# A hybrid decoder step on one core: rows gathered in float32, the last tile's norm inside its selection, merged rows in the gates' place, buffer 5 loaded at the merge

## The chip, the cores and the metric

The kernel runs on one core of one Trainium2 chip, as one launch. The metric is the device time of one execution in microseconds. Before the change it is 1523.48 us, the median of 3 runs (1522.27 to 1524.48).

## The reference

One step of a decoder layer is computed for 256 prompt rows and 8 x 4 sample rows of width 1024, 288 rows in all, everything in float32. The two groups differ only in their states:

```
x @ w_in -> q, f, v, g, z, xBC, dt, gate_a, gate_b
out_a = (rms_norm(hgrn2 recurrence) * sigmoid(g)) @ hg_proj
out_b = rms_norm((mamba-2 recurrence + skip) * silu(z)) @ ssd_proj
merged = sigmoid(gate_a) * out_a + sigmoid(gate_b) * out_b
mix = merged @ w_out
h = layer_norm(ALPHA * x + mix, ln1_g, ln1_b)

logits = h @ router_w + router_b            # 32 experts
top 4 of them, gates = softmax of the top 4 logits
for each chosen expert: gu = h @ w_gu[e] + b_gu[e]; act = (clip(up) + 1) * min(gate, 7) * sigmoid(1.702 * gate)
                        y += gates * (act @ w_down[e] + b_down[e])
x = layer_norm(ALPHA * h + y, ln2_g, ln2_b)
```

The recurrent states and the last three rows before the convolution are outputs too. The change touches what lies between `merged` and the expert products, and the storage of the sum behind them.

## The kernel before

The program is written per engine: each engine has one list of instructions in order, and semaphores join them. An engine whose instruction waits holds up everything behind it. SyncE (SP) issues all the large transfers, on one queue, in the order in which they are written; each also waits for the semaphore that says that its place in memory is free.

Rows lie in three tiles, two of 128 prompt rows (0 and 1) and one of 32 sample rows (2). Up to about 548 us the kernel computes the projections, the two recurrences and the two branches. `gA` and `gB` hold the activated gates, transposed (features across partitions). For each of 8 feature groups the second branch's product is multiplied by `gB` (line 1612), then the first branch's by `gA`, and the sum is written over `gB`, which is called `mT` from there on (lines 1623 and 1624, semaphore `g_m`, called merged_ready).

**The mix.** TensorE multiplies the merged rows by the two halves of `w_out`, in the order of `MIX` (line 697): tile 2 first half, tile 0 first half, tile 2 second, tile 0 second, tile 1 first, tile 1 second (`mix(0)` to `mix(5)`, line 2215). VectorE's `evict(j)` (line 1639) adds ALPHA times the input row (`xres`, loaded again) and writes the sum to `xtok`; TensorE's `turn` (line 2231) transposes that sum, ACT copies it to `hTr`, and TensorE multiplies it with the router's weights (`logits`). Layer norm is folded into the router by factors, so the logits don't wait for the normed rows. The normed rows themselves come from `weigh` (subtract the mean, multiply by `lnw`) and `normal` (multiply by the inverse deviation, add `lnb`), written over `xres`. Ahead of `evict(0)` VectorE waits for the inputs (`g_xr`) and for both vectors of the norm (line 1697, `g_ln` at 32, called ln_parameters_loaded). `choose` finds the 4 experts of each row.

**The blocks.** The chosen (row, expert) pairs are sorted by expert into blocks of 64 rows, of which this input has 32. VectorE writes `psel`, a 0/1 matrix that says which row is in which place of the block; TensorE gathers a block by multiplying the rows by it. A bf16 0/1 matrix times float32 rows isn't exact in one bf16 product, so the rows are held as three bf16 parts `hp` whose sum is the row: ACT casts, GpSimd subtracts the cast from the row, ACT casts what is left, and so on. For tile 2 the three parts lie below each other in 96 partitions (`hp2`), so one product of each half is enough; tiles 0 and 1 take three. For tile 1 TensorE forms the residual itself, with a product by the identity and one by the negated identity `nidb` (lines 2285 to 2290), and VectorE forms the third part (line 1747). The two halves of the 1024 columns go to the two halves of the partitions of one PSUM bank (`gather`, line 2294).

For each block TensorE works through six pieces of 2 MB of the expert's weights: four of `w_gu` (256 rows each) and two of `w_down` (512 rows each). During piece 3 or before piece 4 it gathers the next block's rows, transposes gates, activation and rows, and in every second block, from the third on, it multiplies the pair's outputs back to their rows (`scatter`). SyncE loads the pieces into ten buffers (`buf_kb`, line 620). The first ten pieces, of experts 0 and 1, which nearly every input starts with, are loaded before the table of blocks is known: buffers 0 to 3 around the branches, 4 behind `w_out`, 6 after `mix(4)`, 5 and 7 after `mix(5)`, 8 after the logits and the normed first half of tile 1, 9 after the casts of tile 0. From the eleventh piece on, a ring of nine buffers is used, and a piece is issued when TensorE has used the one that was in its buffer (line 868, `m_f`). After the last block the sum in `yacc` is normed and stored.

The functions that the diff touches, with those that call them:

Of the kernel before, what the change touches and what calls it, by code (L numbers as in the profile page):

```python
# [14 lines left out]
BF16 = mybir.dt.bfloat16  # L15
I32 = mybir.dt.int32
U32 = mybir.dt.uint32
ALU = mybir.AluOpType
# [71 lines left out]
def build(nc, x_prompt, x_sample, state_hgrn, state_ssm, state_conv, hg_lower_bounds, w_in, hg_norm_w, hg_proj,  # L90
# [24 lines left out]
    with ctx:  # L115
# [377 lines left out]
        mT = gB  # L493
# [4 lines left out]
        lnb = at("lnb", 170, [P, D])  # L498
# [98 lines left out]
        t_c, t_r, t_q = S("h_part_cast"), S("h_residual_ready"), S("last_h_residual_ready")  # L597
        t_z = S("last_h_part_ready")
# [49 lines left out]
        hp0 = [[at(f"hp{t}{i}", kb, [P, D], BF16) for i, kb in enumerate(places)] for t, places in enumerate(((148, 150, 152), (162, 164, 114)))]  # L648
        hp2 = at("hp2", 112, [96, D], BF16)
        hres = at("hres", 183, [P, D])  # L650
        yacc = at("yacc", 154, [P, 2, D])
# [10 lines left out]
        psel = at("psel", 205.9375, [P, 3, BLK], BF16)  # L662
# [10 lines left out]
        nidb = at("nidb", 198.6875, [P, P], BF16)  # L673
# [12 lines left out]
        lnw2 = at("lnw2", 148, [P, D])  # L686
        lnb2 = at("lnb2", 162, [P, D])
        lnw4 = at("lnw4", 152, [P, 256])
        lnb4 = at("lnb4", 153, [P, 256])
# [45 lines left out]
        with nc.Block() as block:  # L735
            @block.sync
            def _(sp):
# [74 lines left out]
                sp.dma_start(lnb[:], row(ln1_b[0])).then_inc(g_ln, 16)  # L812
# [76 lines left out]
                for t in range(2):  # L889
                    for h in range(2):  # L890
                        sp.wait_ge(f_y, 2 * t + h + 2)
                        sp.dma_start(y_prompt[0, P * t:P * t + P, CW * h:CW * h + CW], yacc[:, t, CW * h:CW * h + CW]).then_inc(s_out, 16)
# [7 lines left out]
            def _(pool):  # L900
# [53 lines left out]
                pstep(g.tensor_scalar(nidb[:], ident[:], -1.0, None, ALU.mult))  # L954
# [11 lines left out]

                h2 = xres[0:96, 2, :]
                pool.wait_ge(t_c, 1)
                g.tensor_tensor(hres[0:96, :], h2, hp2[:], ALU.subtract).then_inc(t_r, 1)
                pool.wait_ge(t_c, 3)  # L970
                pool.wait_ge(t_r, 1)
                g.tensor_tensor(hres[64:96, :], hres[64:96, :], hp2[64:96, :], ALU.subtract).then_inc(t_r, 1)
                for i in range(2):
                    for n in range(2):
                        cols = slice(CW * n, CW * n + CW)
                        pool.wait_ge(t_c, 6 if i == 0 else 7 + n)
                        pool.wait_ge(t_r, 2 + 2 * i + n)
                        g.tensor_tensor(hres[:, cols], hres[:, cols] if i else xres[:, 0, cols], hp0[0][i][:, cols], ALU.subtract).then_inc(t_r, 1)
# [9 lines left out]
            def _(act):  # L988
# [213 lines left out]
                def cast(t, i, n, residual):  # L1202

                    cols = slice(CW * n, CW * n + CW)
                    act.wait_ge(t_r, residual)
                    a.copy(hp0[t][i][:, cols], hres[:, cols]).then_inc(t_c, 1)

# [3 lines left out]
                act.wait_ge(t_h, 1)  # L1211
                a.copy(hp2[:], xres[0:96, 2, :]).then_inc(t_c, 1)
# [3 lines left out]
                act.wait_ge(t_r, 1)  # L1216
                for band in bands[1:3]:
                    a.copy(hp2[band, :], hres[band, :]).then_inc(t_c, 1)
                for n in range(2):
                    act.wait_ge(t_h, 2 + n)  # L1220
                    a.copy(hp0[0][0][:, CW * n:CW * n + CW], xres[:, 0, CW * n:CW * n + CW]).then_inc(t_c, 1)
# [1232 lines left out]
```

## Time and profile before

| what | value |
|---|---|
| median of 3 runs | 1523.48 us |
| their range | 1522.27 to 1524.48 us |
| profiled execution, its own time | 1523.85 us |
| profiled execution, span of the trace | 1522.1 us |
| TensorE busy (matmul) | 1460.3 us, 96% |
| VectorE busy | 519.5 us, 34% |
| ACT busy | 263.2 us, 17% |
| GpSimd busy | 114.0 us, 7% |
| mean granted clock of TensorE | 0.996 of full |
| bytes moved by DMA | 507.80 MB, mean 334 GB/s |

The times of the table are of one profiled execution, except for the first two rows. Busy shares say little on their own here: the program has stages with different limits, and matmuls are pipelined, so that TensorE can look busy while it waits a little before each one. The chain of waits, followed back from the last instruction, is 61% TensorE's and 25% DMA's, of which the gate-up weights are 23%.

### The profile page before, as it was taken

Reading aid. Unit: us, or ns where it says so; the run is one execution under the profiler, and the core shown is the slowest. Engines: PE = TensorE matmul, PEld = TensorE weight load, DVE = VectorE, ACT = ScalarE, POOL = GpSimd, SP = SyncE. Lnnn points to the kernel's source line nnn. Section 1 sums busy time; section 2 is a strip of 40 time slices with the busy share of each in tenths; the row PEclk is TensorE's granted clock in tenths of the full one; section 3 lists DMA queues with packets and bytes.
Section 4 is the critical chain, followed back from the end, with each engine's and each line's share of the span. In section 5 each row is a group of like instructions: output and inputs, shape, how many; then the busy total and the mean of one; then the engine's idle time right before and its main releaser. Section 6 shows DMA issues by size and latency. Waiting matters only on the chain.

```text
span 1522.1 us, 23099 instructions
## 1 busy us (share of the span) xinstructions
PE 1460.3 (96%) x9252; PEld 743.2 (49%) x9253; DVE 519.5 (34%) x980; ACT 263.2 (17%) x604; POOL 114.0 (7%) x100
## 2 busy tenths in 40 slices
PE   9999999999999998999999999999999999999896
PEld 7777776556777764333333333333333333333332
DVE  3652788767510146122122212211212112122123
ACT  1224214631210014100101101011001001100102
POOL 1002141010502402000000000000000000000000
PEclk9999999999999999999999999999999999999999
DMA  6346686556269647999999999999999999999995
GB/s 211 111 166 176 206 269 232 177 175 193 80 217 333 252 168 310 428 428 427 428 427 429 428 428 429 428 429 428 428 429 428 429 428 428 429 428 429 428 428 217
DMA packets 110285, 507.80 MB, mean 334 GB/s; under 512 B 12552, under 2 KB 49008, under 8 KB 85552
## 3 DMA queue, kind: packets, MB, share of 16 engines
q1 hardware_dynamic: 103548, 499.37, 81.9%
q10 hardware_dynamic: 6676, 7.56, 1.6%
q8 instruction: 46, 0.75, 0.2%
q14 instruction: 15, 0.12, 0.0%
HBM read 491.18 MB, written 15.72 MB: 333 GB/s over the span
## 4 chain that ended last, share of the span: by engine, by line
PE 61%; DMA 25%; DVE 3%; ACT 1%; issue 1%; DVEq 0%; SPq 0%; ACTq 0%
DMA wGU<-in_w_gu 23%; PE ps L2388 12%; PE ps L2393 11%; PE ps L1892 10%; PE ps L2375 5%; PE ps L2196 3%; PE ps L1906 3%; PE ps L2210 2%; PE ps L2302 2%; PE ps L2223 2%; PE ps L2336 2%; PE ps L2310 1%; DMA ringS<-in_ssd_proj 1%; ACT xs L1261 1%; PE ps L2323 1%
## 5 line engine op out<-in xcount | busy, mean ns | idle before, releaser
L2388 PE MATMUL ps<-wGU,xe 128*64 128x512 f32 x1536 | 342.2, 594 | 17.8 <-DMA wGU<-in_w_gu 17.1
L2393 PE MATMUL ps<-wD,aT 128*64 128x512 f32 x1024 | 226.8, 595 | 0.0
L2388 PEld LDWEIGHTS ps<-wGU,xe 128*64 128x64 f32 x1536 | 107.9, 137 | 233.4 <-issue 198.1
L1892 PE MATMUL ps<-xT,ring 128*128 128x288 f32 (+1 forms) x864 | 179.8, 409 | 1.2 <-PEq L200 0.7
L1892 PEld LDWEIGHTS ps<-xT,ring 128*128 128x128 f32 (+1 forms) x864 | 125.1, 170 | 46.0 <-issue 3.5
L2393 PEld LDWEIGHTS ps<-wD,aT 128*64 128x64 f32 x1024 | 70.7, 137 | 131.8 <-issue 127.9
L2375 PE MATMUL ps<-wGU,xe 128*64 128x512 f32 x512 | 121.3, 594 | 11.9 <-DMA wGU<-in_w_gu 11.9
L1785 DVE TENSOR_SCALAR sg<-sg 128x512 f32<-128x512 f32 x32 | 13.7, 427 | 334.3 <-ACT sg L1256 334.3
L1792 DVE COPY ysb<-ps 64x512 f32<-64x512 f32 x32 | 22.2, 694 | 304.8 <-PE ps L2397 304.8
L1256 ACT ACTIVATE sg<-ps 128x512 f32<-128x512 f32 x32 | 19.1, 597 | 470.2 <-PE ps L2380 470.2
L396 PE MATMUL ps<-xT,ring 128*128 128x288 f32 x320 | 78.1, 407 | 0.0
L2375 PEld LDWEIGHTS ps<-wGU,xe 128*64 128x64 f32 x512 | 36.4, 136 | 81.5 <-issue 78.4
L396 PEld LDWEIGHTS ps<-xT,ring 128*128 128x128 f32 x320 | 60.6, 190 | 17.1 <-issue 0.5
L2196 PE MATMUL ps<-ynT,ringS 128*128 128x288 f32 x256 | 62.5, 406 | 0.9 <-DMA ringS<-in_ssd_proj 0.9
L2336 PE MATMUL ps<-ysb,gT 128*128 128x512 f32 x128 | 59.4, 606 | 0.0
L1906 PE MATMUL ps<-ring,xT 128*64 128x512 f32 (+1 forms) x192 | 57.8, 595 | 0.0
L2196 PEld LDWEIGHTS ps<-ynT,ringS 128*128 128x128 f32 x256 | 48.6, 190 | 14.7 <-DMA ringS<-in_ssd_proj 1.4
L1268 ACT COPY ysb<-ps 64x512 f32<-64x512 f32 x32 | 18.5, 578 | 212.9 <-PE ps L2397 212.9
L1768 DVE TENSOR_TENSOR yacc<-yacc,ps 128x512 f32<-128x512 f32 x60 | 41.3, 688 | 22.8 <-PE ps L2336 22.8
L2302 PE MATMUL ps<-hp,psel 128*64 128x512 bf16 x396 | 48.6, 378 | 0.2 <-DVE hp L1747 0.2
L2336 PEld LDWEIGHTS ps<-ysb,gT 128*128 128x128 f32 x128 | 22.9, 189 | 35.1 <-issue 35.1
L2310 PE MATMUL ps<-ident,xs 128*128 128x128 f32 x132 | 24.6, 308 | 10.2 <-ACT xs L1261 9.5
(476 smaller groups left out, 1442.6 us busy)
## 6 DMA issues: line engine op xcount, KB each, us to landing
wGU<-in_w_gu SPq DMA_DIRECT2D x128, 2048.0 KB, 37.0
wD<-in_w_down SPq DMA_DIRECT2D x64, 2048.0 KB, 37.0
ring<-in_w_in SPq DMA_DIRECT2D x21, 2048.0 KB, 9.3
out<-hst SPq DMA_DIRECT2D x8, 1024.0 KB, 5.8
ringS<-in_ssd_proj SPq DMA_DIRECT2D x4, 2048.0 KB, 11.1
wbuf<-prompt_A_rows ACTq DMA_DIRECT2D x16, 384.0 KB, 3.9
out<-Sb SPq DMA_DIRECT2D x2, 2048.0 KB
ring<-in_hg_proj SPq DMA_DIRECT2D x2, 2048.0 KB, 8.6
```

Of the source, the lines that this page charges most:

```text
L396: last = m.matmul(ps[:, 4 + mt, 0:T], ring[n][:, k, mt * P:(mt + 1) * P], xT[:, k, :], start=(k == 0), stop=(k == KD - 1))
L1768: v.tensor_tensor(y, y, p, ALU.add).then_inc(m_sa, 1)
L1892: last = m.matmul(ps[h, b, 0:T], ring[c % 2][:, k, n * P + h.start:n * P + h.stop], xT[:, k, :], start=(k == 0), stop=(k == KD - 1))
L1906: last = m.matmul(ps[h, b, :], xT[:, k, t0 + h.start:t0 + h.stop], ring[c % 2][:, k, :], start=(k == 0), stop=(k == KD - 1))
L2196: last = m.matmul(ps[:, 7 - c % 2, 0:T], ringS[n % 2][:, k, (c % 2) * P:(c % 2) * P + P], ynT[:, k, :], start=(k == 0), stop=(k == XT_ - 1))
L2210: last = m.matmul(ps[:, 4 + c % 2, 0:T], ring[n][:, k, (c % 4) * P:(c % 4) * P + P], onT[:, k, :], start=(k == 0), stop=(k == HH - 1))
L2302: last = m.matmul(ps[half[h], B_X, :], psel[:, t, :], hp0[t][i][:, CW * h:CW * h + CW], start=False, stop=(t == 1 and i == 2))
L2310: last = m.transpose(ps[:, B_XT, f * P:(f + 1) * P], src[:, f // 2, f % 2, :], ident[:])
L2336: return m.matmul(ps[:, bank, :], gT[:, t * P:(t + 1) * P], ysb[j % 2][:], start=True, stop=True)
L2375: last = m.matmul(ps[half[h], bank, :], xe[:, 2 + k, 1, :], wgu[n][:, k, col + CW * h:col + CW * h + CW], start=False, stop=False)
L2388: last = m.matmul(ps[half[h], bank, :], xe[:, f, hx, :], wgu[n][:, k, col + CW * h:col + CW * h + CW], start=(i == 0 and k == 0), stop=False)
L2393: last = m.matmul(ps[half[h], B_Y, :], aT[:, k, i - 4, :], wdn[n][:, k, CW * h:CW * h + CW], start=(i == 4 and k == 0), stop=False)
```

## The change

- **Gather in float32.** `psel` becomes float32 and the gather multiplies the normed rows in `xres` directly: one product for each half and tile, 6 for a block instead of 14 in bf16. The bf16 parts `hp0`, `hp2`, `hres`, the negated identity, ACT's casts, GpSimd's subtractions and the identity products are gone, with their semaphores, and so are the two copies of tile 2's normed rows.
- **The last tile's norm inside its selection.** For the first block tile 1's rows aren't normed yet: `xres[1]` holds only (row - mean) times `lnw`. `psel1` is `psel` times the inverse deviation, and the gather adds two products: `psel` with `lnb`, and `psel1` with `xres[1]`. `normal(1)` runs on VectorE after the first gather. The second half of `weigh(1)` goes behind `choose(2, 1, 2)`.
- **Merged rows in the gates' place.** `mT` is `gA` instead of `gB`. The sum of mix and input goes to three new buffers `mixed` instead of `xtok`. VectorE also waits for the parts of the expert biases (`t_b3`) before the first eviction, since `mixed` lies where they were made.
- **lnb** moves to the place at 148 KB, and its load goes from the early group to behind the eighth merged row.
- **Buffer 5** is loaded there too, right behind it, instead of after `mix(5)`. Buffer 9 comes before 8: 9 after the logits and tile 0's norm, 8 after the last `weigh`.
- **First block.** The copy of the gathered rows and their transposing are cut into halves, and the first products wait only for the first half.
- `yacc` becomes two buffers, filled by ACT after `normal(1)`; the second norm's vectors go over `xres`.

```diff
-        mT = gB
+        mT = gA
-        lnb = at("lnb", 170, [P, D])
+        lnb = at("lnb", 148, [P, D])
+        mixed = [at(f"mixed{t}", kb, [P, D]) for t, kb in enumerate((184, 170, 188))]
...
-        yacc = at("yacc", 154, [P, 2, D])
+        yacc = [at(f"yacc{t}", kb, [P, D]) for t, kb in enumerate((148, 112))]
-        psel = at("psel", 205.9375, [P, 3, BLK], BF16)
+        psel = at("psel", 152, [P, 3, BLK])
+        psel1 = at("psel1", 152.75, [P, BLK])
...
                 sp.dma_start(lnw[:], row(ln1_g[0])).then_inc(g_ln, 16)
-                sp.dma_start(lnb[:], row(ln1_b[0])).then_inc(g_ln, 16)
                 ssd_weights(2)
...
                 piece(0, 4, 4, m_w[4])
+                sp.wait_ge(g_m, KD)
+                sp.dma_start(lnb[:], row(ln1_b[0])).then_inc(g_ln, 16)
+                piece(0, 5, 5, m_w[5])
                 sp.wait_ge(g_mx, 5)
                 piece(1, 0, 6, m_w[6])
                 sp.wait_ge(g_mx, 6)
-                piece(0, 5, 5, m_w[5])
                 piece(1, 1, 7, m_w[7])
                 sp.wait_ge(t_lg, 3)
-                sp.wait_ge(t_h, 5)
+                sp.wait_ge(t_h, 3)
+                piece(1, 3, 9, m_w[9])
+
+                sp.wait_ge(t_h, 4)
                 piece(1, 2, 8, m_w[8])
-
-                sp.wait_ge(t_c, 10)
-                piece(1, 3, 9, m_w[9])
...
                 act.wait_ge(m_x, 1)
-                a.copy(xs[:], ps[:, B_X, :]).then_inc(m_xs, 1)
+                a.copy(xs[:, 0:CW // 2], ps[:, B_X, 0:CW // 2]).then_inc(t_x, 1)
+                a.copy(xs[:, CW // 2:CW], ps[:, B_X, CW // 2:CW]).then_inc(m_xs, 1)
+                act.wait_ge(t_xt, 1)
+                a.copy(xe[:, 0:2].rearrange("p f h j -> p (f h j)"), ps[:, B_S, 0:CW // 2]).then_inc(t_x, 1)
                 act.wait_ge(m_xt, 1)
-                a.copy(xe[:].rearrange("p f h j -> p (f h j)"), ps[:, B_XT, :]).then_inc(m_xc, 1)
+                a.copy(xe[:, 2:4].rearrange("p f h j -> p (f h j)"), ps[:, B_XT, CW // 2:CW]).then_inc(m_xc, 1)
...
                 dve.wait_ge(g_xr, 48)
                 dve.wait_ge(g_ln, 32)
+                dve.wait_ge(t_b3, 1)
                 evict(0)
...
-                dstep(normal(2, slice(0, D)))
-                v.tensor_copy(xres[32:64, 2, :], xres[0:32, 2, :])
-                v.tensor_copy(xres[64:96, 2, :], xres[0:32, 2, :]).then_inc(t_h, 1)
+                normal(2, slice(0, D)).then_inc(t_h, 1)
...
-                for cols in both:
-                    dstep(weigh(1, cols))
+                weigh(1, both[0])
                 scales(2, 1)
                 choose(2, 1, 2)
-                dstep(v.memset(blocks[:, 0:1], 0.0))
-                for cols in both:
-                    normal(1, cols).then_inc(t_h, 1)
+                v.memset(blocks[:, 0:1], 0.0)
+                weigh(1, both[1]).then_inc(t_h, 1)
+                dve.wait_ge(t_h, 4)
...
+                dstep(v.tensor_tensor(psel[:], jcol1..., dsel..., ALU.is_equal))
+                v.tensor_scalar(psel1[:], psel[:, 1, :], var[:, 1:2], None, ALU.mult).then_inc(m_p, 1)
...
+                dve.wait_ge(m_x, 1)
+                for cols in both:
+                    normal(1, cols).then_inc(t_h, 1)
...
+                def gather(t, sel, x, final=False):
+
+                    rows = TILES[t][1]
+                    for h in range(2):
+                        last = m.matmul(ps[half[h], B_X, :], sel[0:rows], x[0:rows, CW * h:CW * h + CW], start=(t == 2), stop=final)
+                    if final:
                         last.then_inc(m_x, 1)
+                def rows_of_block():
+
+                    for t in (2, 0, 1):
+                        gather(t, psel[:, t, :], xres[:, t, :], final=(t == 1))
...
                 pe.wait_ge(m_p, 1)
-                gather(2)
-                gather(0)
+                for t in (2, 0):
+                    gather(t, psel[:, t, :], xres[:, t, :])
                 pe.wait_ge(t_eb, 1)
                 m.matmul(ps[0:1, 3, 0:64], ebc[0:64, 0:1], ident[0:64, 0:64], start=True, stop=True).then_inc(t_tb, 1)
-                pe.wait_ge(t_z, 2)
-                gather(1)
+                gather(1, psel[:, 1, :], lnb)
+                gather(1, psel1, xres[:, 1, :], final=True)
+                pe.wait_ge(t_x, 1)
+                turn_x(range(0, 2), B_S, t_xt)
                 pe.wait_ge(m_xs, 1)
-                turn_x()
+                turn_x(range(2, 4))
```

## Rows read from the trace of the kernel before

**Rows 1.** The page's 40 slices: what the DMA moved in each.

```profile
GB/s 211 111 166 176 206 269 232 177 175 193 80 217 333 252 168 310 428 428 427 428 427 429 428 428 429 428 429 428 428 429 428 429 428 428 429 428 429 428 428 217
```

**Rows 2.** The chain of waits, 546 to 700 us: start, us, what.

```profile
556.62 0.36 PE ps L2238 x4
...
580.84 3.65 PE ps L2223 x8
...
596.69 0.86 PE ps L2302 x6
...
599.68 10.52 PE ps L2388 x48
...
614.07 0.22 PE ps L2298 x2
614.29 1.30 PE ps L2302 x12
...
625.08 10.30 PE ps L2388 x48
...
650.27 3.44 PE ps L2388 x16
...
679.81 10.30 PE ps L2388 x48
```

**Rows 3.** TensorE's waits from 1000 us on: us in total, times, longest.

```profile
PE ps L2388 <- DMA wGU<-in_w_gu: 17.1, 17, 1.2
PE ps L2375 <- DMA wGU<-in_w_gu: 11.9, 9, 1.3
```

**Rows 4.** The chain of waits, from 1485 us: last gate-up load, last expert product.

```profile
1450.78 39.89 DMA wGU<-in_w_gu
...
1505.68 0.23 PE ps L2397 x2
```

**Rows 5.** VectorE's timeline, 545 to 612 us: start, us, line, operation, shapes.

```profile
549.73 1.17 DVE L1647 SCALAR_TENSOR_TENSOR xtok<-xres,ps 32x128 f32<-32x128 f32 x4 [0.57 <-PE ps L2226]
...
586.52 1.54 DVE L1662 SCALAR_TENSOR_TENSOR xres<-xtok,nmu,lnw 128x512 f32<-128x512 f32 x2
...
590.55 1.41 DVE L1676 SCALAR_TENSOR_TENSOR xres<-xres,var,lnb 128x512 f32<-128x512 f32 x2
...
594.00 0.36 DVE L1740 TENSOR_TENSOR psel<-jcol,dsel 128x192 bf16<-128x192 f32 x1
```

**Rows 6.** Single loads by line: issue (ns, at us), then landing; the fifth landing: 604 to 700.

```profile
L805 SPq DMA_DIRECT2D wD<-in_w_down x1: 591/591/591, 548.1 to 548.1; - x1
DMA to landing us min/median/max: 12.9/12.9/12.9
...
L805 SPq DMA_DIRECT2D wGU<-in_w_gu x1: 340/340/340, 573.8 to 573.8; - x1
DMA to landing us min/median/max: 7.9/7.9/7.9
...
L805 SPq DMA_DIRECT2D wD<-in_w_down x1: 351/351/351, 603.5 to 603.5; - x1
DMA to landing us min/median/max: 9.5/9.5/9.5
...
L805 SPq DMA_DIRECT2D wGU<-in_w_gu x1: 333/333/333, 646.8 to 646.8; - x1
DMA to landing us min/median/max: 10.3/10.3/10.3
...
DMA to landing us min/median/max: 9.8/12.6/17.1
...
L812 SPq DMA_DIRECT2D lnb<-in_ln_b x1: 432/432/432, 458.5 to 458.5; - x1
DMA to landing us min/median/max: 11.6/11.6/11.6
```

**Rows 7.** A window: us; busy and count of PE, PEld, DVE, ACT, POOL; PEclk, DMA share, GB/s.

```profile
591.36:594.45 3.09, 2.87 (x3) 1.33 (x5) 2.88 (x9) 1.76 (x3) 0.00 (x0) 0.50 1.00 422
```

More of the change, by code:

```diff
@@ L685, in build @@
         selq = at("selq", 100.25, [P, P])
[L686 to L689, printed above, removed]
+        lnw2 = at("lnw2", 154, [P, D])
+        lnb2 = at("lnb2", 158, [P, D])
+        lnw4 = at("lnw4", 162, [P, 256])
+        lnb4 = at("lnb4", 163, [P, 256])
         fsum = at("fsum", 207.75, [P, 8])
@@ L965, in _ @@
                 g.sem_inc(t_b3, 1)
[L967 to L978, printed above, removed]
                 pool.wait_ge(m_x, 1)
@@ L1215, in _ @@
                 root(1)
[L1216 to L1221, printed above, removed]
-                act.wait_ge(t_r, 2)
-                a.copy(hp2[64:96, :], hres[64:96, :]).then_inc(t_c, 1)
                 turned(3)
-                cast(0, 1, 0, 3)
-                cast(0, 1, 1, 4)
+                act.wait_ge(t_h, 1)
                 for q in range(4):
@@ L1276, in _ @@
                 act.wait_ge(f_c, 1)
-                a.activation(lnq[:], yacc[:, 0, :], ACT.Square, bias=mu2[:, 0:1], accum_out=fsq[:, 0:1]).then_inc(f_v, 1)
+                a.activation(lnq[:], yacc[0][:], ACT.Square, bias=mu2[:, 0:1], accum_out=fsq[:, 0:1]).then_inc(f_v, 1)
                 act.wait_ge(f_m, 1)
@@ L1283, in _ @@
                 act.wait_ge(f_c, 2)
-                a.activation(lnq[:], yacc[:, 1, :], ACT.Square, bias=mu2[:, 1:2], accum_out=fsq[:, 1:2]).then_inc(f_v, 1)
+                a.activation(lnq[:], yacc[1][:], ACT.Square, bias=mu2[:, 1:2], accum_out=fsq[:, 1:2]).then_inc(f_v, 1)
                 for j in range(3):
@@ L2237, in turn @@
                         k = 4 * n + c
-                        last = m.transpose(ps[:, b, c * rows:(c + 1) * rows], xtok[0:rows, t, k * P:(k + 1) * P], ident[0:rows, 0:rows])
+                        last = m.transpose(ps[:, b, c * rows:(c + 1) * rows], mixed[t][0:rows, k * P:(k + 1) * P], ident[0:rows, 0:rows])
                     last.then_inc(t_ht, 1)
@@ L2283, in _, with turn_x @@
                 m.matmul(ps[:, 7, 32:64], trib[:], msk[:, 1, :], start=False, stop=True).then_inc(t_cm, 1)
[L2285 to L2303 removed]
+                half = [slice(0, BLK), slice(BLK, 2 * BLK)]
+                def gather(t, sel, x, final=False):
[3 more added lines that the diff above has]
+                    if final:
                         last.then_inc(m_x, 1)
[L2306 removed]
+                def rows_of_block():
+                    for t in (2, 0, 1):
+                        gather(t, psel[:, t, :], xres[:, t, :], final=(t == 1))
+                def turn_x(fs=range(4), bank=B_XT, done=m_xt):
                     src = xs[:].rearrange("q (i p k) -> q i k p", i=2, k=2)
[L2309 to L2311 removed]
+                    for f in fs:
+                        last = m.transpose(ps[:, bank, f * P:(f + 1) * P], src[:, f // 2, f % 2, :], ident[:])
+                    last.then_inc(done, 1)
                 def turn_a():
@@ L2343, in scatter, with run @@
                         (prompt(j, B_S + j % 3) if j < 4 else samples(B_S + j % 3)).then_inc(m_s, 1)
-                def run(b, turn0, first, pair, places=None):
-                    pe.wait_ge(m_xc, b + 1)
+                def run(b, turn0, first, pair, places=None, head=False):
+                    if head:
+                        pe.wait_ge(t_x, 2)
+                    else:
+                        pe.wait_ge(m_xc, b + 1)
                     for i in range(6):
+                        if head and i == 1:
+                            pe.wait_ge(m_xc, 1)
                         n, loaded = (first + i) % RING, turn0 * 64 + 16 * ((first + i) // RING + 1)
@@ L2358, in run @@
                             pe.wait_ge(m_xs, b + 1)
-                            for t in (2, 0, 1):
-                                gather(t)
+                            rows_of_block()
                             if pair is not None:
```

80 lines of the change are left out of this document (19 added, 61 removed).

## The prediction, made before the result was known

> **What bounds the kernel now.** I read the slices of the page first. From slice 16 on (about 590 us) the DMA moves 427 to 429 GB/s in every slice until the last one [rows 1]: 32 blocks of six 2 MB pieces of expert weights, one piece every 4.9 us. The ring has nine buffers, so the second question is who waits for whom. The chain of waits shows the rhythm of TensorE: block 0 starts at 599.68 us, block 1 at 625.08, block 2 at 650.27, block 3 at 679.81 [rows 2]. A block without scatter takes 25.2 us, one with it 29.5, and 17 of the one and 15 of the other make 871 us. From the first block to the last matmul of the last (1505.9) it really is 906.2. The difference, 35 us, is TensorE waiting for weights, and the waits view finds such waits only after 1000 us, 29 us in two rows (modelled ends of matmuls overhang, so they come out short) [rows 3]. So the expert stage has two clocks that run close together: the stream of pieces, which is the one that ends the run, and TensorE, which has only 35 us in hand over 32 blocks. From the landing of the last gate-up piece (1490.67) until its last product ends (1505.9), TensorE's own work is the path, a gather as in block 0 included [rows 4].
>
> Ahead of that stage the chain is TensorE's without a break: the turning of the first output tile at 556.62, the last half of w_out's products until 584.49, then VectorE's norm and choice, the selection, the gather and block 0 [rows 2].
>
> **The change, part by part.** All sums are made against the profiled execution: span 1522.1 us, time 1523.85. The median of the three timed runs is 1523.48, so a shift of the span is added to the median as it is. About 0.2% (3 us) is what a measurement of this kernel tells from no change.
>
> *The bias vector lnb.* Its load leaves the early group and stands on SyncE behind the down piece into buffer 4, after the wait for the eighth merged row. VectorE still waits for 32 counts of ln_parameters_loaded before its first eviction, which ran at 549.73 [rows 5]; TensorE's third step there, the turning at 556.62, waits for that eviction, and everything behind it on TensorE (mix(2) to mix(5)) is queued behind it. When does lnb land? The down piece is issued at 548.1 and lands 12.9 us later, at 561.0; a piece issued into an empty queue needs 7.9 (573.8) [rows 6]. It lay behind w_out's second half. lnb, issued at about 549.2, lies behind both. The old lnb load, with other loads ahead of it, took 11.6 us for its 512 KB [rows 6]. At 428 GB/s it adds 1.2 us behind the piece: landing 562.2. Then the eviction of 1.17 us, and TensorE goes on at 563.5 instead of 556.6: a stall of 6.9 us. Bounds: 5.7 if it lands with the piece, 8 if as much as 2 us later. Nothing else can run on TensorE meanwhile, since its queue is in order; VectorE has slack to catch up, as its work on these tiles is shorter than w_out's products.
>
> The Trainium skill, "DMA: Bandwidth & Descriptors", section "Queues, rings and completion order", says that completion is not FIFO per issuing engine. Taken for this load it would let lnb land before the piece. The same section says that each ring takes its descriptors in order; the 12.9 us beside 7.9 agree with that.
>
> *TensorE's clock.* When TensorE idled around 588 us, the granted clock was 0.50 of full (1.2 of 2.4 GHz) and stayed so for 3.1 us after dense work began again at 591.36 [rows 7]. A stall of 7 us will be followed by the same: 3.1 us at half speed cost 1.5 us. Bounds: 0 and 3.
>
> *Tile 2's copies, the casts and the residuals* (two copies of 0.7 us on VectorE, ACT's casts, GpSimd's six subtractions). None stands on the chain before 584.49; taking them away is worth nothing there. TensorE's last eviction point moves with the stall alone.
>
> *The stretch from w_out's last product to block 0.* Before: 584.49 to 599.68, 15.2 us. Half of the last tile's weigh (1.54 for two) goes behind the choice: the mask is ready 0.77 earlier. Behind it stands one half of weigh (0.77) where two halves of normal (1.41) stood: 0.64 saved. The selection ended 594.36; now 592.95, and 0.2 more for psel1 (a guess between 0.1 and 0.36, the cost of psel itself), so 593.2 [rows 5]. Gone are the two identity products, the casts between and the subtraction (between selection and the gather's end they leave 597.55 as it was [rows 2]). In their place stand 8 float32 calls of 512 columns (tiles 2, 0, and 1 twice, two halves each). One costs two instructions of 0.215: block 0's first three gate-up pieces are 48 in 10.3 to 10.5 us [rows 2]. That is 3.4 us, and 0.2 for the block table, at full clock. But TensorE has been idle as it was at 588, now with no products to wake it, so 1.5 is added as above: gather ready at 598.4. The halved copy and turning then take four short steps of about 0.3 instead of 2.1: about 1.3. Block 0 at 599.7 against 599.68: nothing gained, +0.1. Bounds: -1.7 (clock high at once) and +1.7 (low throughout). SyncE's release follows the table row, which comes about 3 us before block 0; it does not bind.
>
> So block 0 starts 6.9 + 1.5 + 0.1 = 8.5 us later: 608.2. Bounds 4 and 12.7.
>
> *Buffer 5 at the merge.* It moves 4.9 us of transfer out of the busy stretch after 584.5 into the hole behind w_out. But the eleventh piece may be issued only when block 0 has used its first: 603.5, 3.9 after block 0's start, landing 9.5 later because others were still ahead [rows 6]. With one fewer ahead it lands after 7.9: 612.0 + 7.9 = 619.9 against 613.0, so the stream is 6.9 us late. That is all that buffer 5 gives: 1.6 us. The order of pieces 9 and 8 changes nothing, both land before 612.
>
> *The gathers of every block.* Before, 14 bf16 instructions take 1.52 us (0.22 and 1.30 [rows 2]); two halves run side by side, 0.217 a pair. After, 6 float32 calls are 12 instructions of the form of the gate-up products: 12 x 0.215 = 2.58. That is 1.06 us more a block, 34 in all, against 35 in hand. Most of it is hidden, but not at both ends. At the start the queue of pieces is short: the piece issued at 646.8 lands 10.3 later. After, the stream stands 1.6 nearer and its issue is two gathers (2.1) later: 6.6 us, less than the 7.9 it needs, so the stream slips 1.3. The next tight place is a block on, with about the same time in hand (least 9.8 in this stretch [rows 6]) and three gathers behind: 1.2 again. Then the queue is long. Together 2.5. At the end the last block's gather is on the path, between that landing and the last product: 1.1 more [rows 4]. TensorE's own sum gives 8.5 + 34 - 35 = 7.5, less than the stream's, so the stream stays the bound.
>
> Sum: 6.9 + 2.5 + 1.1 = +10.5 us. Span 1532.6, median 1534.0. With the bounds of block 0's start and no slip at the low end: 4.0 - 1.6 + 1.1 = +3.5 to 12.7 - 1.6 + 3.6 = +14.7.
>
> **Rivals.**
> *lnb lands in time*, past the piece that is ahead of it: no stall, no cold clock there. Block 0 at 599.8, the stream 1.5 earlier, slip 2.5 and tail 1.1: +2.1, 1525.6. For it: it is a small load issued 7 us before it is needed. Against: the piece ahead of it was itself kept back by 5 us. 9%. This is where the Trainium skill's sentence on completion order, above, would lead.
> *Faster: the freed 4.9 us of transfer shorten the stream*, since it is the bound from 584.5 on. Then -4.9 + 1.1 = -3.8: 1519.7. Its point is the issue of the eleventh piece: it must come 4.9 us before 603.5, so block 0 must start by about 594.8, and no stall may stand ahead. Against: the stretch above gives nothing, and the selection alone ends at 593.2. 4%.
> *Float32 gathers at bf16's pace a call* (12 halves side by side in 0.7): no slip, tail -0.9: 6.9 - 0.9 = +6.0, 1529.5. Against: same form as gate-up. 4%.
> *The clock stays low for longer, or lnb lands later than 563*: +15 or more, over 1538. 6%.
> The forecast: 77%.
>
> **Numbers.** Predicted 1534.0. The likeliest case has 1529 to 1538 by its bounds trimmed at the ends; the range for 8 in 10 is the same, since it leaves out the first two rivals (13%) and most of the last (5%). Slower by over 0.2% (above 1526.5): forecast, the third, the fourth and a third of the first, 90%. Within 0.2%: two thirds of the first, 6%. Faster: 4%.
>
> **What would show it.** VectorE's first eviction: idle before it until DMA lnb, start near 562; TensorE idle for about 7 us before the turning, and a stretch at 0.50 behind it. w_out's last product ends near 593 instead of 584.5. Block 0 near 608. The gather near 2.6 us a block. A hole in the DMA before the eleventh piece lands near 620. Waits of TensorE for weights shrunk from 29 us to a few, late in the run. The prediction is wrong if lnb lands before 556, if the clock doesn't fall behind the stall, or if TensorE starves as long as before.

## The result and the profile after

After the change the kernel takes 1542.70 us, the median of 4 runs (1542.58 to 1544.62); before it 1522.88 us on the same chip (4 runs, 1521.80 to 1524.48). The ratio is 1.0119, with a 95% interval of 1.0097 to 1.0140: slower, as forecast, but by 19.8 us where 10.5 had been forecast, and outside the range. The profiled execution took 1542.59 us with a span of 1540.9, 18.8 more than the span before. The working below is on spans.

First three lines of the page: the slices of DMA traffic, then section 4, how the chain of waits is shared, then from section 5 the gather's products.

```profile
GB/s 209 110 166 185 209 271 234 182 137 192 124 223 295 271 178 231 428 387 426 427 427 428 428 429 428 429 429 429 429 428 428 428 429 428 429 428 429 429 429 157
...
PE 85%; DVE 3%; issue 2%; ACT 2%; DMA 0%; SPq 0%; DVEq 0%; ACTq 0%
...
L2252 PE MATMUL ps<-xres,psel 128*64 128x512 f32 (+1 forms) x396 | 99.3, 618 | 3.2 <-DVE psel L1703 3.2
```

The DMA is still full all through the blocks, as in [rows 1]. On that row alone one would call the stream the bound again. But the chain is 85% TensorE and no DMA at all, where it had been 61% and 25%. The queue of pieces is busy with transfers that nobody is waiting for yet. TensorE's waits from 540 us to the end (us in total, times, longest) say the same:

```profile
PE ps L2265 <- ACT xs L1224: 9.5, 32, 0.3
PE ps L2199 <- DVE mixed L1610: 6.9, 1, 6.9
PE ps L2252 <- DVE psel L1703: 3.2, 1, 3.2
PE ps L2243 <- DVE msk L1656: 1.9, 1, 1.9
```

No wait for weights is left; the 29 us of [rows 3] are gone. The longest wait is new: 6.9 us before the first turning. The chain, 546 to 714 us (start, us, what), shows where the time went:

```profile
548.21 13.08 issue
561.39 0.28 DVE mixed L1610
...
562.61 0.63 PE ps L2199 x4
563.25 3.49 PE ps L2187 x64
...
588.71 3.65 PE ps L2184 x8
...
600.70 0.27 DVE psel L1703
601.01 3.88 PE ps L2252 x8
...
605.18 3.05 PE ps L2252 x8
...
609.69 10.52 PE ps L2347 x48
...
624.08 2.87 PE ps L2252 x12
...
636.45 10.30 PE ps L2347 x48
...
663.00 3.44 PE ps L2347 x16
...
693.89 10.30 PE ps L2347 x48
```

Against [rows 2] the turning comes at 562.61 instead of 556.62, w_out's last product ends at 592.36 instead of 584.49 (+7.9), and block 0 starts at 609.69 instead of 599.68 (+10.0). From there on, a block without scatter takes 26.55 us (663.00 less 636.45) instead of 25.19, one with scatter 30.89 instead of 29.54: 1.36 more in each, which is the gather, 2.87 instead of 1.52. In 32 blocks that makes 43.5 us, and there were 35 in hand. So the account of this one profiled execution closes:

block 0 later 10.0 + gathers 43.5 - in hand 34.9 = +18.6, against +18.8 of the span.

With no wait for weights left in the blocks, such a sum must come out near the span. What it shows is where the time lies; that TensorE is the bound is shown by the missing waits.

Loads issued between 547 and 549.5 us: what, KB, median us to landing.

```profile
wD<-in_w_down SPq DMA_DIRECT2D x2, 2048.0 KB, 14.8
ring<-in_w_out SPq DMA_DIRECT2D x1, 2048.0 KB, 8.2
lnb<-in_ln_b SPq DMA_DIRECT2D x1, 512.0 KB, 13.4
```

lnb, issued at 547.8, lands at 561.2, and VectorE's first eviction starts at 561.39, where [rows 5] has it at 549.73. The turning is still only 6.0 us later than before, not 6.9, as TensorE reached it 0.9 sooner: its merge products start at 546.65 instead of 547.60. Before the change it had waited for the second branch's weights, which were issued behind lnb; after it that wait is gone. The row of the kernel before:

```profile
PE ps L2196 <- DMA ringS<-in_ssd_proj: 0.9, 1, 0.9
```

The granted clock in three stretches (columns as in [rows 7]):

```profile
559.70:566.50 6.80, 3.89 (x68) 3.46 (x68) 3.19 (x7) 1.55 (x2) 0.00 (x0) 0.50 0.79 330
597.20:607.50 10.30, 6.73 (x18) 1.56 (x20) 4.49 (x19) 0.00 (x0) 0.00 (x0) 0.50 1.01 429
607.50:620.00 12.50, 11.79 (x56) 4.77 (x54) 6.23 (x20) 5.97 (x9) 2.09 (x4) 1.00 0.57 212
```

TensorE works at 1.2 GHz in the first two. The second covers the whole first gather: work starts at 601.01 and the clock is back 6.5 us later.

### The profile page after: what moved, and what is told of

Same layout as the page of the kernel before. It is cut to its first block, busy times and chain, and to the rows that moved or that the text cites. A ratio compares the mean times of both kernels' runs of the same rounds, so it can differ in the third digit from the quotient of the medians.

```text
span 1540.9 us, 22938 instructions
## 1 busy us (share of the span) xinstructions
PE 1502.4 (98%) x9185; PEld 742.5 (48%) x9185; DVE 513.5 (33%) x977; ACT 253.5 (16%) x592; POOL 104.0 (7%) x93
## 4 chain that ended last, share of the span: by engine, by line
PE 85%; DVE 3%; issue 2%; ACT 2%; DMA 0%; SPq 0%; DVEq 0%; ACTq 0%
PE ps L2347 22%; PE ps L2352 15%; PE ps L1853 10%; PE ps L2334 7%; PE ps L2252 6%; PE ps L2157 4%; PE ps L2291 4%; PE ps L1867 3%; PE ps L2171 2%; PE ps L2265 2%; PE ps L2184 1%; ACT xs L1224 1%; PE ps L2278 1%; PE ps L2339 1%; PE ps L1941 1%
## 5 line engine op out<-in xcount | busy, mean ns | idle before, releaser
L2252 PE MATMUL ps<-xres,psel 128*64 128x512 f32 (+1 forms) x396 | 99.3, 618 | 3.2 <-DVE psel L1703 3.2
L2252 PEld LDWEIGHTS ps<-xres,psel 128*64 128x64 f32 (+1 forms) x396 | 22.7, 136 | 70.5 <-issue 67.2
```

The costliest lines, as they stand in the source:

```text
L2252: last = m.matmul(ps[half[h], B_X, :], sel[0:rows], x[0:rows, CW * h:CW * h + CW], start=(t == 2), stop=final)
```

## The experiments

The theory after the result: TensorE ends the run, so that the end is block 0's start plus 32 times whatever a block has in addition, less 35 us. The rival: the stream of pieces ends it, as the forecast had it, and TensorE's additions matter only at the ends. Each median stands beside that of the kernel before on the same chip. Block 0's start and the span are those of one profiled execution, in us; these spans spread by one or two us, so the medians decide what a kernel costs. "After" and "before" name the kernel that was edited.

| kernel | runs | median us | before | ratio, 95% interval | block 0 | span |
|---|---|---|---|---|---|---|
| a_late_wait | 4 | 1533.71 | 1523.47 | 1.0068 (1.0050 to 1.0086) | 600.90 | 1532.1 |
| b_late_lnb | 5 | 1532.74 | 1524.21 | 1.0048 (1.0024 to 1.0071) | 608.17 | 1529.8 |
| a_rows128 | 4 | 1536.50 | 1523.47 | 1.0085 (1.0068 to 1.0101) | 607.73 | 1533.0 |
| a_no_tile0 | 4 | 1537.14 | 1523.47 | 1.0087 (1.0070 to 1.0104) | 611.26 | 1535.6 |
| a_warm | 4 | 1540.77 | 1523.47 | 1.0114 (1.0097 to 1.0131) | 607.40 | 1538.6 |
| b_warm | 10 | 1524.33 | 1523.84 | 1.0001 (0.9992 to 1.0011) | 600.97 | 1524.0 |
| a_all | 10 | 1526.87 | 1523.84 | 1.0016 (1.0006 to 1.0026) | 598.95 | 1525.4 |
| a_all_late5 | 10 | 1525.37 | 1524.21 | 1.0007 (0.9996 to 1.0017) | 598.02 | 1523.6 |
| b_load3 | 5 | 1533.83 | 1523.84 | 1.0060 (1.0043 to 1.0077) | 604.67 | 1539.0 |
| b_load6 | 4 | 1543.68 | 1523.84 | 1.0119 (1.0099 to 1.0139) | 601.76 | 1543.3 |
| b_plus_09 | 10 | 1528.87 | 1524.21 | 1.0037 (1.0022 to 1.0051) | 600.43 | 1526.1 |
| b_plus_13 | 4 | 1540.81 | 1524.21 | 1.0100 (1.0078 to 1.0123) | 600.30 | 1539.4 |

**The stall alone taken out: a_late_wait** (after). lnb gets a semaphore of its own, waited for where it is first read.

```diff
-                sp.dma_start(lnb[:], row(ln1_b[0])).then_inc(g_ln, 16)
+                sp.dma_start(lnb[:], row(ln1_b[0])).then_inc(g_lb, 16)
...
-                dve.wait_ge(g_ln, 32)
+                dve.wait_ge(g_ln, 16)
...
+                dve.wait_ge(g_lb, 16)
                 normal(2, slice(0, D)).then_inc(t_h, 1)
```

> The changed kernel, with a semaphore of its own for lnb, waited for before tile 2's normal instead of before the first eviction; the load itself stays where it is (it landed at 561.2 us). Theory 1 (the stall of 7.0 us and the slow clock behind it, 1.6 us, are passed on one to one, since TensorE is the bound up to the end): first eviction near 549, the turning near 556, no stretch at 0.50 there, block 0 about 8.6 us earlier, time 8.6 us less than the changed kernel, near 1534. Theory 2 (the stream of weights is the bound, and the stall only shifts work that waits later anyway): 0 to 3 us less.

Measured: 9.0 us less than after. The wait of 6.9 is gone and nothing came in its place, no wait for weights either. Its chain:

```profile
600.90 10.52 PE ps L2349 x48
...
615.30 2.87 PE ps L2254 x12
```

Block 0 is 1.2 later than before, and 1.2 + 43.5 - 34.9 = +9.8 against +10.0 of the span. The eleventh piece lands at 612.6, 0.4 earlier than before, and yet the run ends 10 later: here the stream is not what ends it. That the whole 9 came back doesn't by itself decide between the theories, as the next run shows: when the stream is the bound, a delay ahead of it is passed on too.

**The stall alone put in: b_late_lnb** (before). Only the load of lnb is moved, behind the down piece into buffer 4.

```diff
-                sp.dma_start(lnb[:], row(ln1_b[0])).then_inc(g_ln, 16)
                 ssd_weights(2)
...
                 piece(0, 4, 4, m_w[4])
+                sp.dma_start(lnb[:], row(ln1_b[0])).then_inc(g_ln, 16)
```

> The kernel before, with nothing changed but the load of lnb, which stands behind the down piece of buffer 4 as in the change; it is still waited for before the first eviction. Theory 1 (stall of 6.9 us, slow clock 1.6 us, and the stream then resumes 1.5 us nearer to block 0): block 0 8.5 us later, time 7 us more than before, 1530.5. Theory 2 (TensorE or the weights in hand take it up): less than 3 us more.

Its waits of TensorE, then the clock behind the stall:

```profile
PE ps L2388 <- DMA wGU<-in_w_gu: 16.3, 16, 1.2
PE ps L2375 <- DMA wGU<-in_w_gu: 11.9, 9, 1.3
...
PE ps L2238 <- DVE xtok L1647: 7.4, 1, 7.4
```

```profile
559.50:566.30 6.80, 3.63 (x64) 3.33 (x68) 3.19 (x7) 1.55 (x2) 0.00 (x0) 0.50 0.04 14
```

Block 0 starts 8.5 us later, the span is 7.7 longer (the median 8.5, where 7 was expected), and TensorE waits for weights as long as it did before. With bf16 gathers the stream does stay the bound, and a delay ahead of the first ring piece is passed on nearly whole. This kernel differs from before by the one load, and TensorE's merge products start 1.3 us sooner in it too (546.26), with a wait of 0.2 instead of 0.9 for the second branch's weights.

**The gather as it had been priced: a_rows128** (after). Tile 2's product takes 128 rows too (the 96 below the sample rows cleared), so no 32-row product stands between those of 128.

```diff
+                v.memset(xres[32:64, 2, :], 0.0)
+                dstep(v.memset(xres[64:128, 2, :], 0.0))
...
-                dstep(v.tensor_copy(msk[0:96, 2, :], ps[0:96, 6, 0:E_]))
...
-                    rows = TILES[t][1]
+                    rows = P
```

> The changed kernel, with tile 2 gathered by 128 rows instead of 32: rows 32 to 127 of it are cleared, and their choices are not copied from rows 0 to 31, so they add zero. Theory 1 (a float32 call costs 0.43 us a pair of instructions, and what goes beyond that in the gather of 2.87 us comes from the weight loads of 32 rows, which don't run ahead of the product before them, on both sides of tile 2): gather 2.6 us, 0.25 to 0.29 less in each of 32 blocks, 8 to 9 us less in all. Theory 2 (the float32 weight load of psel costs it whatever its rows, or the change from bf16 to float32 does): gather stays at 2.87, time the same or a little more.

Four times the rows, and it is shorter; the time fell by 6.2 us, less than the 8 to 9 expected. First the chain of a_rows128, then its weight loads in one gather (start, us), then the same of the kernel after:

```profile
600.75 3.42 PE ps L2253 x8
...
607.73 10.52 PE ps L2348 x48
...
622.12 2.58 PE ps L2253 x12
```

```profile
648.64 0.14 PEld L2253 LDWEIGHTS ps<-xres,psel 128*64 128x64 f32 x2 [0.29 <-issue]
649.06 0.14 PEld L2253 LDWEIGHTS ps<-xres,psel 128*64 128x64 f32 x2 [0.29 <-issue]
649.49 0.14 PEld L2253 LDWEIGHTS ps<-xres,psel 128*64 128x64 f32 x2 [0.29 <-issue]
```

```profile
650.55 0.19 PEld L2252 LDWEIGHTS ps<-xres,psel 32*64 32x64 f32 x4 [0.63 <-issue]
651.56 0.20 PEld L2252 LDWEIGHTS ps<-xres,psel 128*64 128x64 f32 x4 [0.81 <-issue]
652.04 0.14 PEld L2252 LDWEIGHTS ps<-xres,psel 128*64 128x64 f32 x2 [0.29 <-issue]
```

With 128 rows throughout, a pair of weight loads starts every 0.43 us, the time of the pair of products. Around the 32-row products the loads come in fours with longer gaps (0.63 and 0.81 us), and the gather is 2.87 instead of 2.58: 0.29 a block, 9.3 in all. That the 32 rows cost the 0.29 is shown by the edit; that they do so through the order of the loads is read from these rows. In the first gather the edit did more: the clock came back at 603.8, 3.0 us after work began, where it took 6.5 in the kernel after, and the way from w_out's last product to block 0 is 15.6 us instead of 17.3. Why is not shown. The span is 1533.0, +10.9, but this execution is the fastest of the four; by the medians it is +13.0. Here the stream is the bound again (7% of the chain is DMA, TensorE waits for weights twice, 2.6 us), as TensorE's sum is less: 8.1 + 34.2 - 34.9 = +7.4. The Trainium skill, "TensorE: Matmul & The Clock Gate", section "Why this matters for your kernels", says that a single product over 32 rows takes the time of one over 128. For the product itself the trace of the kernel after agrees (means of 613 and 605 ns); for the sequence it does not, by these 0.29 us.

**The stream's floor: a_no_tile0** (after; blocks 1 to 31 leave out tile 0's two products).

```diff
-                    for t in (2, 0, 1):
+                    for t in (2, 1):
```

> The changed kernel, with the gathers of blocks 1 and on leaving out tile 0's product (so the rows of tile 0 are missing from these blocks): 0.86 us less of TensorE's work in 31 or 32 gathers. Theory 1 (two floors: TensorE's sum, which the change lifted above the stream's by about 8 us, and the stream of pieces, whose first ring piece lands 8 us later than before): TensorE waits for weights again late in the run, and of the 27 us only 8 to 12 show: 1531 to 1535. Theory 2 (TensorE's work alone sets the time now): 27 us less, near 1515.

The gather measured 2.01, so TensorE has 31 x 0.86 = 26.7 us less to do than after, and the time fell by 5.6 only, to 2 us above the expected 1531 to 1535. Its waits:

```profile
PE ps L2334 <- DMA wGU<-in_w_gu: 9.2, 7, 1.3
PE ps L2347 <- DMA wGU<-in_w_gu: 8.3, 7, 1.2
PE ps L2199 <- DVE mixed L1610: 8.0, 1, 8.0
```

Beneath TensorE's sum lies the stream, as the rival says, at +13.5 of span here: block 0 starts at 611.26 (the stall was 8.0 in this run, and the clock came back 7.4 us after the gather began), and TensorE's own sum would be 11.6 + 15.7 - 34.9 = -7.6 (0.49 more a block than before). A faster gather gives nothing beyond that point.

Where the stream is the bound, the traces divide its part. The eleventh piece is the first of the ring; the last gate-up piece's landing is the end of a load in the chain. All as differences from before (613.0, 1490.67 [rows 4], and 31.4 us from there to the end):

| kernel | eleventh piece lands | last gate-up piece lands | lost between them (slip) | end behind it (tail) | span |
|---|---|---|---|---|---|
| a_rows128 | +6.4 | +9.8 | 3.5 | +1.1 | +10.9 |
| a_no_tile0 | +9.8 | +13.0 | 3.2 | +0.5 | +13.5 |
| a_all | -2.5 | +2.2 | 4.7 | +1.1 | +3.3 |
| a_all_late5 | -1.9 | +0.4 | 2.3 | +1.1 | +1.5 |

The loads behind it, of a_rows128 and then of a_all (start and length, whose sum is the landing):

```profile
1461.69 38.83 DMA wGU<-in_w_gu
```

```profile
1454.03 38.83 DMA wGU<-in_w_gu
```

**The clock: a_warm and b_warm.** a_warm (after) keeps TensorE busy with products whose result nobody reads, two behind the last logits and three behind the counts; b_warm (before) does so with 8 and 2 in bf16.

```diff
+                pe.wait_ge(t_h, 3)
+                for _ in range(2):
+                    m.matmul(ps[:, 4, :], ident[:], xres[:, 0, 0:CW], start=True, stop=True)
...
+                for _ in range(3):
+                    m.matmul(ps[:, 4, :], ident[:], xres[:, 0, 0:CW], start=True, stop=True)
```

> The changed kernel, with five products of no use in float32 (128x512, into an idle bank) put where TensorE waits for the last choices and for the selection. Theory 1 (the first gather of 16 instructions took 7.2 us instead of 3.8 because the granted clock was 0.50 from 597.2 to 607.5 us): the clock stays at 1.00, the first gather takes 3.9 us, block 0 is 3 us earlier, time 3 us less. Theory 2 (the gather's length has another cause, or the added products delay it as much): within 1 us.

> The kernel before, with eight bf16 products of no use before the wait for the last choices and two behind the counts. Theory 1 (the clock at 0.50 from 587.6 to 594.5 us cost its identity products 1.7 us, and block 0's start is passed on): clock 1.00, block 0 1 to 1.7 us earlier, time 1 to 1.7 us less than before. Theory 2 (the path there is VectorE's, and the stream was held by pieces still ahead of the eleventh): 0 to 0.6 us less.

a_warm, the clock and then the first gather:

```profile
567.20:620.00 52.80, 50.69 (x226) 24.12 (x220) 29.96 (x96) 10.74 (x22) 2.16 (x4) 1.00 0.56 216
```

```profile
601.76 2.08 PE ps L2257 x8
...
604.05 1.89 PE ps L2257 x8
...
607.40 10.52 PE ps L2352 x48
```

With the clock at 2.4 GHz throughout, the way from w_out's last product (593.1) to block 0 is 14.3 us instead of 17.3. That is what the low clock cost at this place: 3.0. The median is 1.9 lower where 3 was expected; in the profiled run w_out's last product ended 0.8 later than in that of after. The ratios alone, 1.0114 and 1.0119, don't tell the two kernels apart. In b_warm the same way became 14.5 instead of 15.2, but nothing was gained in the median. Its profiled run was 2.0 us late at w_out's end already, so it doesn't show block 0's gain directly; the eleventh piece needed 10.1 us from issue to landing instead of 9.5, so it still lay behind others.

**All three repairs: a_all,** and **a_all_late5,** which puts buffer 5's piece back behind `mix(5)`.

```diff
-                piece(0, 5, 5, m_w[5])
                 sp.wait_ge(g_mx, 5)
                 piece(1, 0, 6, m_w[6])
                 sp.wait_ge(g_mx, 6)
+                piece(0, 5, 5, m_w[5])
```

> The changed kernel with three things at once: lnb waited for at its first use, tile 2 gathered by 128 cleared rows, five idle products that keep the clock. Measured alone they gave 9.0, 6.2 and 1.9 us of the 19 us. Theory 1 (they add until the stream of weights is the bound, which then ends it): block 0 near 598, the eleventh piece lands near 609.5 against 613.0 before the change, the stream then slips 2 to 3 us on the longer gathers of the first blocks, the last block's gather costs 1.1: 1522 to 1524, the same as the kernel before. Theory 2 (they add up fully): 1542.7 - 17 = 1525.6 or more, TensorE without waits for weights. Theory 3 (buffer 5 at the merge then gives its 4.9 us): 1518 to 1519.

> The changed kernel with the three repairs, and the piece of buffer 5 put back behind w_out's last product. Theory 1 (with the repairs the stream is the bound again, and the eleventh piece is ready to be issued at 602.8, so one more piece ahead of it keeps it to 613 instead of 610.5): 2.5 us more than the kernel with the three repairs, 1529.4. Theory 2 (TensorE's work is the bound even with the repairs): the same within 0.5 us.

a_all is 15.8 us faster than after and still 0.16% slower than before, 3 us above the 1522 to 1524 expected; a_all_late5 can't be told from before, and is 1.5 us faster than a_all where it was expected 2.5 slower. The early piece gains nothing that can be seen, though it does what was counted: the eleventh piece lands 7.7 us after its issue in a_all and 9.3 after it in a_all_late5. Both have block 0 ahead of before and a float32 gather of 2.58, and end 1.5 to 3.3 us later by the span: 1.1 of it is the last gather, behind the last landing, and the rest is slip that is larger than what the stream had gained (table above). In a_all the piece issued at 648.2 takes 7.6 us, as into an empty queue: what the stream gained at its first piece, it has lost by then. No version beat the kernel before.

**TensorE's load alone, without the change: b_load3 and b_load6** (before, 6 and 12 more bf16 instructions a block), **b_plus_09 and b_plus_13** (before, one float32 product of 512 columns, or one of 512 and one of 256).

```diff
+                            for _ in range(3):
+                                for h in range(2):
+                                    m.matmul(ps[half[h], B_XT, :], psel[:, 0, :], hp0[0][0][:, CW * h:CW * h + CW], start=True, stop=True)
```

```diff
+                            m.matmul(ps[:, B_XT, 0:512], ident[:], xe[:].rearrange("p f h j -> p (f h j)")[:, 0:512], start=True, stop=True)
+                            m.matmul(ps[:, B_XT, 0:256], ident[:], xe[:].rearrange("p f h j -> p (f h j)")[:, 0:256], start=True, stop=True)
```

> The kernel before, with three more pairs of bf16 products of no use in the gather of every block (0.65 us of TensorE's work a block, 21 us in all). Theory 1 (TensorE has 35 us in hand under the stream): only the last block's 0.65 us shows, 0.5 to 1.5 us more than before. Theory 2 (TensorE's work is the bound throughout): 21 us more.

> The kernel before, with six more pairs of bf16 products in the gather of every block (1.30 us a block, 41.6 us in all, against 1.35 us by which the change lengthened a block). Theory 1 (35 us in hand, then the bound passes to TensorE): 41.6 - 35 = 6.7 us more than before, TensorE waits for weights hardly at all. Theory 2 (the stream stays the bound, as I had forecast for the change): slip 1.6 and tail 1.3, 3 us more. Theory 3: 41.6 more.

> The kernel before, with one float32 product of 128x512 of no use (two instructions, 0.86 us) ahead of every block's gather: 27.5 us in all. The pairs of bf16 products in the two runs of this kind had brought stalls of TensorE of about 2 us at each turn of its loop, which nothing in the trace releases; with fewer instructions they should stay away. Theory 1 (TensorE has 35 us in hand): 0.86 at the end and 0.3 to 0.5 of slip, 1.2 us more than before. Theory 2 (TensorE's work is the bound): 27 us more. Theory 3 (the loop's stall comes with any added instruction): 10 us more or so, with the stall in the trace.

> The kernel before, with a float32 product of 512 and one of 256 columns ahead of every block's gather: 1.29 us a block, 41.3 in all, about what the change adds (1.35). Theory 1: above the 35 us in hand the bound passes to TensorE: 6.3 us more than before, few waits for weights left. Theory 2 (the stream stays the bound): tail 1.3 and slip 1.6, 3 us more. Theory 3: stalls of the loop as in the run with six pairs, 15 to 20 us more.

The first two missed (0.5 to 1.5 and 6.7 us more expected, 10.0 and 19.8 measured), and for a reason that has nothing to do with the sum. b_load6's waits, and its instruction loads between 800 and 1500 us; then the same queue of b_plus_13:

```profile
PE ps L2391 <- issue: 9.5, 5, 2.4
...
PE ps L2329 <- issue: 1.8, 1, 1.8
...
q8 instruction: 36, 0.59, 0.3%
```

```profile
q8 instruction: 1, 0.02, 0.0%
```

TensorE stands for 1.8 to 2.4 us at four places about 175 us apart, and once more at the end of the blocks, released by no semaphore. The queue of instruction loads moves 36 packets in this stretch, and one or none in before, after and the b_plus kernels, which have no such stalls. That the longer loop has to be loaded anew at each turn is inferred from these two rows. The Trainium skill, "Runtime: NRT & Kernel Launch", section "Instruction fetch mechanics", says that a taken branch whose target isn't at hand forces a load before execution goes on; the rows agree, and it did not bear on the change, which made the loop shorter. With 10.6 us of such stalls in b_load6 and 12 in b_load3 (above the 0.7 that before has too), these two kernels measure the load of TensorE badly; b_load3's profiled run is also the slowest of its five. With them b_load6's sum is 2.1 + 41.6 - 34.9 + 10.6 = 19.4, and behind its first stall the granted clock was 0.50 for a while, which cost 1.7 more (5.35 us for 16 products that take 3.65 behind the other stalls), against +21.2 of span.

The b_plus kernels measure it well, though their own expectations missed (1.2 and 6.3 us more than before, against 4.7 and 16.6 by the medians): the products cost more than their 0.86 and 1.29 us. In b_plus_13:

```profile
614.70 1.05 PE ps L2359 x2
615.75 0.43 PE ps L2360 x2
616.18 0.34 PE ps L2298 x2
```

The pair of the gather behind them takes 0.34 instead of 0.22 [rows 2], and the first product 1.05. Between block starts there is 1.17 more in b_plus_09 and 1.61 in b_plus_13. By the theory's sum that makes 0.8 + 37.5 - 34.9 = +3.4 for the one (the span is +4.0) and 0.6 + 51.5 - 34.9 = +17.2 for the other (+17.3). The waits view finds no wait for weights in either. But in b_plus_09 the two bounds meet: its chain goes through a gate-up load again, which lands at 1493.49, 2.8 later than before, and a tail 1.2 longer makes +4.0, so there the stream ends it. The sum held within 0.3 us in the four kernels in which TensorE ends the run (after, a_late_wait, b_plus_13, and a_warm: 7.7 + 43.5 - 34.9 = +16.3, span +16.5). This kernel has 35 us in hand for TensorE, and every microsecond beyond it is paid in full, unless the stream by itself takes longer still.

## Why the prediction was wrong

The direction held. The median is 8.7 us above the forecast, and most of it, 6.2 us, goes once the gather has the length that the forecast gave it (a_rows128). Two smaller terms were off besides, at lnb's stall and on the way to block 0.

- **lnb's stall: right as a wait, but not what it cost.** Forecast: lands at 562.2, stall 6.9, TensorE goes on at 563.5. Measured: 561.2, 6.9 and 562.6. The forecast put the leaving of the early group at nothing. It was worth 0.9 us: everything up to the merge came that much sooner, the piece ahead of lnb as well, so that against before only 6.0 us were passed on. By itself the stall was 7.4 in b_late_lnb, which cost 7.7 of span. The load landed right behind the piece issued before it, 561.2 behind 559.8. Where the Trainium skill says that completion is not FIFO per issuing engine ("DMA: Bandwidth & Descriptors", "Queues, rings and completion order"), lnb did come behind the piece, in after and in b_late_lnb (561.2 behind 560.1), and the rival built on that fell.
- **The clock behind the stall: right in the mechanism.** Forecast 1.5, measured 1.9: 1.6 in products that took 3.49 us instead of 1.89, 0.3 in the turning ahead of them (0.63 instead of 0.36).
- **From w_out's end to block 0: too low by 2.** Forecast +0.1, at most +1.7; measured 17.3 against 15.2, +2.1. VectorE's part came 1.3 us sooner (8.6 us from w_out's end to psel1's, instead of 9.9; 1.2 were counted), but the clock stayed at 0.50 for 6.5 us after work began, where 3 had been taken from [rows 7], and the eight calls cost 3.97 at full clock (a_warm) instead of 3.4. Block 0 came at 609.7 and not 608.2: 6.0 + 1.9 + 2.1 = 10.0 later, where 6.9 + 1.5 + 0.1 = 8.5 had been forecast. In a_rows128 the clock did come back after 3.0 us and the way was 15.6, 0.4 above before, so this miss too goes with the 32-row products.
- **Buffer 5 at the merge: right,** 1.8 us at the eleventh piece (7.7 to landing instead of 9.5, forecast 7.9, a gain of 1.6), and nothing at the end of the run.
- **The gathers: this step failed.** It read "6 float32 calls are 12 instructions of the form of the gate-up products: 12 x 0.215 = 2.58". Two of the six calls are not of that form: tile 2 has 32 rows. Measured 2.87, and 2.58 exactly once the rows are 128 (a_rows128). The 0.29 is 9.3 us in 32 blocks. The text had 34 us against 35 in hand and concluded "TensorE's own sum gives 8.5 + 34 - 35 = 7.5, less than the stream's, so the stream stays the bound". With 43.5, and block 0 at +10.0, it is 18.6, and TensorE is the bound. A sum within 3 us of the other one did not allow an error of a tenth in the gather's length, and the range did not say so: its upper end was made of the stream's bounds alone.
- **The stream's part: about right where the stream is the bound.** a_rows128 is the kernel that the forecast had in mind. Its profiled span is +10.9 against +10.5 forecast, but by the medians it is +13.0, so part of that agreement is luck. In the span the eleventh piece is 6.4 late (forecast 6.9), the slip is 3.5 (forecast 2.5) and the tail 1.1 (forecast 1.1).
- **What would show it:** the text named "Waits of TensorE for weights shrunk from 29 us to a few". They are zero, and the gather stood in the chain at 2.87 rather than 2.6. These two rows by themselves point to the cause.

Three things stay open: why the slip is 4.7 us in a_all and 2.3 in a_all_late5, why the clock came back so much sooner in a_rows128, and what the change would give with bf16 gathers kept in the loop and float32 only in the first. That was not tried: the bf16 parts and the early piece need the same place in memory.

## What to carry to other kernels

Where two engines run close together, write down both sums with their slack, and put the error of every term through both: a term hidden under one clock costs its full excess once it lifts the other over it. Price an added instruction by the row of its own shape, partitions included, or by bounds that hold its absence; "same form" must mean the rows, the columns of the weights and the columns of the data. A load that is moved back takes with it every wait that counts it: give it a semaphore of its own and wait at its first reader (here 9 of the 20 us lost).

## What the runs showed of the hardware

- A float32 product over 32 rows between products over 128 costs as much itself (613 and 605 ns), but a gather of 12 such instructions took 0.29 us longer than one with 128 rows throughout (2.87 and 2.58). Clearing the other 96 rows once and using 128 is cheaper.
- After a spell of little work the granted clock stayed at 0.50 for 6.5 us of further work in after, 7.4 in a_no_tile0 and 7.7 in a_late_wait, all beginning with 32-row products, and for about 3 us in a_rows128 and before [rows 7]; five idle float32 products in the spell kept it at 1.00 and saved 3.0 us.
- Six more instructions a block (b_load3), and TensorE stalled four times in the loop for about 2 us each, with 36 packets on the queue of instruction loads instead of none or one; two to four more did nothing of the kind.
- A pair of bf16 products behind a float32 one took 0.34 us instead of 0.22 (b_plus_09, b_plus_13).
